# A transformer block pair with expert retrieval on one core: second projections of heads 2 and 3 placed among the first picks, blocks fetched once, head 1's selection earlier, sums on four column tiles

## The reference

```
q = (h2 @ w_query)                       # 8 heads, two halves of 128
s = q . sub_keys                         # 128 scores for each half
v1, i1 = top 16 of half 0; v2, i2 = top 16 of half 1
best = top 16 of all 256 sums v1 + v2    # 16 experts for each token and head
act = gelu(u[expert] . h2)
out += softmax(best) * act * v[expert]
```

## Time and profile before

| | |
|---|---|
| three runs | 1752.94, 1753.07, 1755.21 us (median 1753.07) |
| the profiled execution | 1749.33 us, its span 1747.5 us |
| TensorE matmul busy | 1595.6 us (91%) |
| TensorE weight load busy (beside the matmuls) | 742.7 us (42%) |
| VectorE / ScalarE / GpSimd busy | 750.2 / 500.7 / 288.6 us |
| TensorE's mean granted clock | 0.967 of full |
| moved by DMA | 595.22 MB, mean 341 GB/s |
| SyncE's issues into the ring | 160 (18 of `w_mod` and `w_in`, 142 of packed blocks, of which 8 come in two parts) |
| row fetches from GpSimd | 256 |

### The profile page before, as it was taken

How to read it: one execution, slowest core, us unless ns; L and a number is a source line. 1 busy time by engine, 2 the same in 40 slices (tenths; PEclk the granted TensorE clock), 3 DMA queues, 4 the chain that set the end, 5 groups by cost and what they waited for, 6 DMA issues and landing times.

```text
span 1747.5 us, 15554 instructions
## 1 busy us (share of the span) xinstructions
PE 1595.6 (91%) x5460; PEld 742.7 (42%) x5460; DVE 750.2 (43%) x1807; ACT 500.7 (29%) x1283; POOL 288.6 (17%) x268
## 2 busy tenths in 40 slices
PE   6999998499579997897999988999999999999998
PEld 3444464165134542243443333344344444455443
DVE  3653155866785556646525446542312100031101
ACT  3311224322432323314344134334412110122210
POOL 1000002323533333313212212221000000000000
PEclk8999999799889998999999999999999999999999
DMA  9555349999999999999999999999877677855784
GB/s 353 203 182 193 144 181 382 421 392 421 421 404 410 415 421 421 422 421 421 419 421 420 421 421 421 420 416 421 334 289 272 231 301 269 313 216 226 288 299 181
DMA packets 94958, 595.22 MB, mean 341 GB/s; under 512 B 7025, under 2 KB 7025, under 8 KB 28193
## 3 DMA queue, kind: packets, MB, share of 16 engines
q1 hardware_dynamic: 56576, 319.28, 46.6%
q0 software_dynamic: 37584, 270.75, 37.6%
q10 hardware_dynamic: 720, 4.19, 0.6%
HBM read 593.15 MB, written 1.05 MB: 340 GB/s over the span
## 4 chain that ended last, share of the span: by engine, by line
PE 79%; DMA 11%; DVE 5%; ACT 2%; issue 2%; SPq 1%; POOL 0%; DVEq 0%; POOLq 0%; ACTq 0%
PE bank L975 36%; PE bank L1136 10%; PE bank L1053 8%; DMA arena<-in_peer_rows,pidx 7%; PE bank L684 7%; PE bank L761 3%; PE bank L951 3%; PE bank L940 2%; DMA ring<-in_weights 2%; PE bank L982 2%; DVE arena L2080 2%; DMA ring<-in_w_mod 1%; PE bank L738 1%; PE bank L654 1%; SPq L594 1%
## 5 line engine op out<-in xcount | busy, mean ns | idle before, releaser
L1610 POOL DMA_INDIRECT arena<-in_peer_rows,pidx x227 | 252.3, 1112 | 582.9 <-PE bank L1136 520.7
L1136 PE MATMUL bank<-arena,keep 128*32 128x512 f32 x908 | 264.2, 661 | 71.8 <-ACT keep L1568 71.8
L975 PE MATMUL bank<-ring,arena 128*128 128x512 f32 x736 | 319.4, 593 | 0.0
L2080 DVE SCALAR_TENSOR_TENSOR arena<-arena,ring 128x1024 f32<-128x1024 f32 x227 | 272.6, 1223 | 90.8 <-DMA arena<-in_peer_rows,pidx 88.6
L975 PE MATMUL bank<-ring,hT_all 128*128 128x512 f32 x544 | 239.3, 595 | 3.7 <-issue 3.4
L975 PEld LDWEIGHTS bank<-ring,arena 128*128 128x128 f32 x736 | 138.5, 190 | 168.8 <-issue 168.7
L975 PEld LDWEIGHTS bank<-ring,hT_all 128*128 128x128 f32 x544 | 101.3, 190 | 135.1 <-issue 133.0
L1136 PEld LDWEIGHTS bank<-arena,keep 128*32 128x32 f32 x908 | 50.3, 116 | 215.2 <-issue 119.6
L1555 ACT ACTIVATE pf<-pf 128x2 f32<-128x2 f32 x128 | 25.8, 202 | 374.6 <-DVE arena L2080 334.5
L2195 DVE TENSOR_TENSOR x_all<-x_all,bank 128x512 f32<-128x512 f32 x40 | 27.5, 688 | 205.7 <-PE bank L1053 112.2
L684 PE MATMUL bank<-ring,hT_all 128*128 128x512 f32 x192 | 87.2, 611 | 3.1 <-DMA ring<-in_w_in 1.6
(11 more groups left out here) (374 smaller groups left out, 1704.7 us busy)
## 6 DMA issues: line engine op xcount, KB each, us to landing
ring<-in_weights SPq DMA_DIRECT2D x126, 2048.0 KB
ring<-in_w_mod SPq DMA_DIRECT2D x12, 2048.0 KB
ring<-in_w_in SPq DMA_DIRECT2D x6, 2048.0 KB
ring<-in_weights SPq DMA_DIRECT2D x8, 1024.0 KB
ring<-in_weights SPq DMA_DIRECT2D x8, 512.0 KB
arena<-in_peer_rows,pidx POOLq DMA_INDIRECT x227
mem_all<-in_b_mod POOLq DMA_DIRECT2D x3, 512.0 KB, 9.6
hT_all<-in_xT ACTq DMA_DIRECT2D x1, 1024.0 KB, 7.2
```

Source lines behind the costliest of these rows:

```text
L975: m = mm(b[:, :], src[:, k], slot8[w][:, k], start=(k == 0), stop=(k == KC - 1))
L1136: m = mm(acc[b][r:r + 32, :], diag[n % 8], vslot[n % SLOTS][:, b * 512:(b + 1) * 512], start=(n % 128 < 4), stop=(n % 128 >= 124))
L1610: nc.gpsimd.indirect_dma_start(out=row_in[n % SLOTS], out_offset=None, in_=a["peer_rows"], in_offset=bass.IndirectOffsetOnAxis(ap=pidx[:, ...
L2080: stt(uslot[n % SLOTS], uslot[n % SLOTS], 1.0, h2g[n % 4], ALU.mult, ALU.mult, accum_out=pact2[:, 16 * (g % 2) + k:16 * (g % 2) + k + 1]). ...
```

## The change

It has these parts:

1. `weight_plan` drops `out_again` and `wq_again`. The new order after the modulation and projection blocks is out 1, out 0, wq 0, mod 10, mod 11, wq 1, wq 2, wq 3, in slots 1, 0, 2, 3, 3, 0, 1, 2. A block stays until the second tile has used it: out 0 until the second tile's first half of the projection, out 1 until its second half, wq 0 until query q11, wq 1 until q13.
2. TensorE's stream before the picks loses the queries q02 and q03 and key scores 02 and 03, and gets the second tile's product with out 0 (`out_half(1, 0..3)`) between the transposes mr1 and md1. The modulation rows 10 move up by several steps, and their copy goes to VectorE; that of the transpose at11 goes to ScalarE. The product with out 1 comes at pick 4, q02 at 6, k02 and q03 at 8, k03 at 10.
3. VectorE selects the halves and best pairs of head 1 before the first row products; the rest of head 1 follows after picks 0 to 7, head 2 after picks 10 to 15 (the new table `first`, one entry for each pair).
4. In the sum of a pick pair the second half of the columns goes to partitions 32 * ((n + 2) % 4), so that the four matmuls use four column tiles. `add_experts` reads that half back crosswise in two instructions of 64 partitions.
5. At the start `keep_warm` issues five matmuls of 512 columns whose result nobody reads, and `dist` (1 MB) is issued by SyncE after the fifth block, not by ScalarE as its third DMA.
6. The final norm: the product of the lower half with its gain moves ahead of the last feed-forward product (new step `gain 0`), and on the upper half gain and scale are one instruction.
7. `gate_exp` of groups 1 and 2 moves up on ScalarE.

```diff
-EARLY_PLACES = (0, 1, 2, 0, 1, 3, 1, 2, 0, 1, 2, 0)
+EARLY_PLACES = (1, 0, 2, 3, 3, 0, 1, 2)
...
-    for name, i in (("out", 1), ("out", 0), ("wq", 0), ("wq", 1)):
+    for name, i in (("out", 1), ("out", 0), ("wq", 0)):
         block(name, i)
     rows("mod", 10)
     rows("mod", 11)
-    for name, i in (("out", 1), ("out", 0), ("wq", 0), ("wq", 1)):
-        block(name + "_again", i, name)
-    block("wq", 2)
-    block("wq", 3)
+    for i in (1, 2, 3):
+        block("wq", i)
...
-PICK_WORK = {0: ["out 1"], 4: ["out 0"], 8: ["regroup 1"], 16: ["h2_turns 1"],
+PICK_WORK = {4: ["out 1", "regroup 1"], 6: ["query q02"], 8: ["keys 02", "query q03"], 10: ["keys 03"], 16: ["h2_turns 1"],
...
@@ sync @@
+                if n == 5:
+                    sp.dma_start(s_all[:, 0:2048], a["dist"]).then_inc(sem("dist_in"), 16)
...
-            act.dma_start(s_all[:, 0:2048], a["dist"]).then_inc(sem("dist_in"), 16)
...
@@ tensor @@
+            def keep_warm(n):
+
+                for _ in range(n):
+                    mm(M[0][:, :], ones, h2_all[:, 0:512], start=True, stop=True)
...
             feature_sums("nc", squares_c, sem("squares_ctx"), ones)
+            keep_warm(1)
...
             mod_rows(0, cpad)
+            keep_warm(3)
             mod_rows(2, cpad)
             mod_columns(0)
             mod_columns(2)
+            keep_warm(1)
...
             diff_turn(1, 0)
+            mod_rows(10, cpad)
             ret_values(1, 0)
...
             diff_values(1, 0)
-            mod_rows(10, cpad)
             mod_rows(11, cpad)
...
-            query("q02", 2, slice(0, P))
             pe.wait_ge(sem("mix_ret"), 2)
             turn_blocks(turn("mr1"), [PR[:, 1, c * P:(c + 1) * P] for c in range(4)])
             repeat_tokens(0, 2)
-            key_scores(0, 2)
+            repeat_tokens(0, 3)
+            open_unit("o1a")
+            open_unit("o1b")
+            out_half(1, range(0, 4))
             pe.wait_ge(sem("mix_diff"), 2)
             turn_blocks(turn("md1"), [PR[:, 1, 2048 + c * P:2048 + (c + 1) * P] for c in range(4)])
-            repeat_tokens(0, 3)
-            query("q03", 3, slice(0, P))
-            key_scores(0, 3)
...
-                        r = 32 * (n % 4)
+                        r = 32 * ((n + 2 * b) % 4)
...
@@ vector @@
             mix_ret(1, 2)
+            half_top(1, 0)
+            half_top(1, 1)
+            best_pairs(1)
             out_mean(3)
-            key_copy(0, 2)
+            next_pairs(1)
             mix_diff(1, 3)
-            mix_turn("md", 1)
-            key_copy(0, 3)
...
-                    link(tt(part, acc[half][:, :], g5row[:, c], ALU.mult))
+                    if half == 0:
+                        link(tt(part, acc[0][:, :], g5row[:, c], ALU.mult))
+                    else:
+                        for to, at in ((0, 64), (64, 0)):
+                            q = tt(part[to:to + 64], acc[1][at:at + 64, :], g5row[at:at + 64, c], ALU.mult)
+                        link(q)
...
-            then = {(0, 0): [lambda: half_top(1, 0), lambda: half_top(1, 1)],
-                    (0, 1): [lambda: best_pairs(1), lambda: next_pairs(1), lambda: pair_rows(1, 0), lambda: pair_rows(1, 1), lambda: spread(1), lambda: residual_out(1)],
-                    (0, 2): [lambda: select(1), lambda: h2_mean(1), lambda: half_top(2, 0), lambda: half_top(2, 1), lambda: best_pairs(2), lambda: next_pairs(2)],
-                    (0, 3): [lambda: h2_apply(1), lambda: pair_rows(2, 0), lambda: pair_rows(2, 1), lambda: spread(2)],
+            first = [[lambda: mix_turn("md", 1), lambda: pair_rows(1, 0), lambda: pair_rows(1, 1)], [lambda: spread(1)], [],
+                     [lambda: residual_out(1), lambda: select(1)], [], [lambda: h2_mean(1), lambda: key_copy(0, 2), lambda: half_top(2, 0), lambda: half_top(2, 1)],
+                     [lambda: h2_apply(1), lambda: best_pairs(2), lambda: next_pairs(2)],
+                     [lambda: key_copy(0, 3), lambda: pair_rows(2, 0), lambda: pair_rows(2, 1), lambda: spread(2)]]
...
+                elif kind == "gain":
...
+                    dve.wait_ge(tile_squares[t], i + 1)
+                    low = x[:, t, 0:512]
+                    tt(low, low, frow[:, 0:512], ALU.mult).then_inc(sem("final_gained"), 1)
...
-                    tt(low, low, frow[:, 0:512], ALU.mult).then_inc(sem("final_gained"), 1)
-                    tt(high, high, frow[:, 512:D], ALU.mult).then_inc(sem("final_gained"), 1)
...
-                    ts(high, high, rs, None, ALU.mult).then_inc(sem(f"tile{t}_done1"), 1)
+                    stt(high, high, rs, frow[:, 512:D], ALU.mult, ALU.mult).then_inc(sem(f"tile{t}_done1"), 1)
```

More of the change, by code:

```diff
@@ L233 @@
 for _w, _us, _lag in STEPS:
-    AFTER_ROWS += [(0, _fill) for _fill in FILLS.get(_w, ())] + [(1, _w)]
+    for _fill in FILLS.get(_w, ()):
+        AFTER_ROWS += [(0, "gain 0")] * (_fill == "final 0") + [(0, _fill)]
+    AFTER_ROWS += [(1, "gain 0")] * (_w == "dn1 5") + [(1, _w)]
 SEQUENCE = [(0, _w) for _w in UNDER_ROWS] + AFTER_ROWS
@@ L302 @@
          + [(n, 1) for n in ("at00", "at01", "m4", "m5", "at02", "at03", "m6", "m7", "md0", "mr0")] + [("h20", 2)]
-         + [(n, 1) for n in ("at10", "at11", "m10", "m11", "at12", "at13", "mr1", "md1")] + [("h21", 2)])
+         + [(n, 1) for n in ("at10", "m10", "at11", "m11", "at12", "at13", "mr1", "md1")] + [("h21", 2)])
 def turn(name):
@@ L559, in wait_released @@
                 eng.wait_ge(turn_ready, turn(f"m{i}") + 1)
-            elif (name, i) == ("out_again", 1):
+            elif (name, i) == ("out", 0):
                 eng.wait_ge(sem("out_half_used"), 1)
@@ L731, in out_half @@
             def out_half(t, ks):
+                first, last = (0, 7) if t else (4, 3)
                 for k in ks:
                     if k % 4 == 0:
-                        w = weights(piece["out_again" if t else "out", k // 4])
+                        w = weights(piece["out", k // 4])
                         turned(turn(("mr" if k == 0 else "md") + str(t)))
@@ L738, in out_half @@
                         m = mm(bank[unit(f"o{t}" + "ab"[half]) % 4][:, :], mixT[t][:, k], slot4[w][:, k % 4, half * 512:(half + 1) * 512],
-                               start=(k == 4), stop=(k == 3))
-                        if k == 3:
+                               start=(k == first), stop=(k == last))
+                        if k == last:
                             m.then_inc(unit_ready, 1)
-                        elif k == 7 and half and t:
+                        elif k == 3 and half and t:
                             m.then_inc(sem("out_half_used"), 1)
@@ L751, in query @@
             def query(name, h, cols_of):
-                w = weights(piece["wq_again" if name[1] == "1" and len(name) == 3 else "wq", h // 2])
+                w = weights(piece["wq", h // 2])
                 b = open_unit(name)
@@ L1396, in _ @@
             out_root(3)
-            query_copy("q02", ("k00",))
             mix_turn("mr", 1)
@@ L1400, in _ @@
             repeat_copy(0, 3)
-            query_copy("q03", ("k01",))
+            gate_exp(1)
             def memory_copy(l, u):
@@ L1423, in g5_move @@
                 f(g5row, g5early, ACT.Copy).then_inc(sem("g5_moved"), 1)
-            after = {8: [lambda: h2_square(1)], 10: [lambda: h2_root(1)],
+            after = {6: [lambda: query_copy("q02", ("k00",))], 8: [lambda: h2_square(1), lambda: query_copy("q03", ("k01",))], 10: [lambda: h2_root(1)],
+                     14: [lambda: gate_exp(2)],
                      16: [lambda: h2_turn(1)], 18: [lambda: query_copy("q10")], 20: [lambda: query_copy("q11")],
@@ L1467, in layer_step @@
                       accum_out=ss).then_inc(tile_squares[t], 1)
+                elif kind == "final":
+                    i, ss, ms, sd, rs = tile_stats(t, "final")
                     act.wait_ge(tile_squares[t], i + 1)
@@ L1549, in _ @@
                             repeat_copy(1, i)
-                    if n0 == 8:
-                        gate_exp(1)
-                    if q == 6 and g + 2 < 16:
+                    if q == 6 and 0 < g < 14:
                         gate_exp(g + 2)
@@ L2279, in _ @@
                     dots(n0, n0 + 2)
+                    for work in first[j] if g == 0 else ():
+                        work()
                     if j % 2:
```

27 lines of the change are left out of this document (11 added, 16 removed), and 5 rows, old and new, of tables (UNITS, last_unit).

## The result

The changed kernel takes 1738.49 us in the median of six runs (1737.36 to 1739.77), the kernel before 1753.51 beside it: ratio 0.9914, 95% interval 0.9902 to 0.9927. That is 15 us faster. The forecast was 1729; 1738 is the time given for rival A. The profiled execution took 1737.44 us, its span 1735.6.

What follows compares the result with a forecast made beforehand. DMA bytes were taken to bound the picks until 1128 us, except in windows where TensorE held DMA back, and TensorE after that. 2.5 + 5.5 + 6.2 + 9 + 0.7 = 23.9 us off 1753.1 gave 1729 us, range 1715 to 1742.

Steps and rivals of the forecast that it cites:

- rival A: Stretch after 1128 us: DMA holds it too, so the gain of 9 us goes; 1738 us, chance 18%.
- The start of the picks: From the first row fetch to 350 us: four weight blocks fewer bring 5.5 us (0 to 10).
- the gap: Near 288 us: DMA idles about 3 us because fetches 7 and 8 wait for the transpose md1.
- The two dips: 350 to 370 and 510 to 530 us: shorter sums let DMA regain 2.6 MB, 6.2 us (0 to 7).
- rival D: Picks: TensorE's gaps bring half-clock restarts; after 1128 us they undo the 9 us and cost 6; 1744 us, 5%.
- The last stretch: After 1128 us: TensorE is the bound, 13 shorter sums save 12.0 us, taken as 9 (0 to 12).
- lead of 15 us: After 1128 us: weights up to three blocks, 15 us, ahead of TensorE cover a stretch shorter by 12 us.
- The front: Before the picks: dist moved lands a w_mod block earlier, idle matmuls speed the projection; 2.5 us (0 to 3).
- The final norm: Between mean and reciprocal on VectorE: two products leave this place, gain 0.7 us (0.4 to 1.2).
- B: Picks: bytes count in full, no DMA gap at 287, all 12 us after 1128; 36 us, 1717 us, 14%.
- C: Pair sums: four tiles share the array only in pairs, so their saving is absent; 1744 us, chance 5%.
- E: Picks: 8 us stands with all row slots landed idle DMA; four make it slower, 1761 us, chance 4%.

Runs made afterwards that it cites:

- e1: Changed kernel with the old pair sum on two column tiles and the old add_experts; 1743.88 us, ratio 0.9957 to the kernel before.
- e12: Changed kernel with the transpose md1 moved ahead of the product with out 0; 1733.86 us, ratio 0.9911 to the kernel before.
- e9: Changed kernel with the old two-tile sum for the last 13 pair sums (picks 230 to 255); 1740.00 us, ratio 0.9935 to the kernel before.
- e10: Changed kernel with picks 228 to 243 fetched as 4 KB rows instead of 8 KB; 1729.64 us, ratio 0.9886 to the kernel before.
- e3: Changed kernel without the five idle matmuls and with dist back on ScalarE's queue; 1740.91 us, ratio 0.9945 to the kernel before.
- e6: Changed kernel without the five idle matmuls, dist at its new place; 1737.37 us, ratio 0.9930 to the kernel before.
- the third set: Follow-up runs on one chip, among them the changed kernel unaltered once more: 1738.70 us, ratio 0.9933 to the kernel before.
- e2: Kernel before with only the new four-tile sum and the new add_experts; 1747.96 us, ratio 0.9978 to the kernel before.

## Why the prediction was right in sign and 9 us too low

The sum was 2.5 + 5.5 + 6.2 + 9 + 0.7.

- **The start of the picks, 5.5 forecast:** e1's lead of 5.1 us over its fetch 0 agrees. The byte count held, the gap too: forecast 3 us near 288; measured 221 GB/s at 290 to 295, which is 2.4 us. But it came later than I had it: the product with out 0 began at 284.76 for 283.5 and VectorE's mix_turn at 292.34 for 291, as TensorE ran at half clock before (at 273.39 us 16 records in 3.64 us, which take 1.92 at 278.52). And that gap may be worth more than the 3 us I gave it: e12 removes it and has 3.4 us more in the traces and 0 to 4.8 by the runs. One sentence of this step was wrong at the root: modulation rows 10 moved up "delay" select and cost 0.8 us. I looked at TensorE's and VectorE's order only; the move opens the slot for rows 11, and without it 7.6 us or more are lost. My total escaped this by luck, since I hadn't seen the shared slot either.
- **The two dips, 6.2 forecast:** 350 to 370 is filled, worth 2.7 us of lead in the byte count (4.9 to 7.6). Against e1 it is more: over their own fetch 0 the changed kernel has 9.7 us at fetch 236 and e1 5.0, 4.6 us for the tiles up to there. 510 to 530 isn't: with 290 and 412 GB/s it misses (131 + 9) x 10 us, 1.4 MB or 3.3 us, as much as before. In front of it TensorE stands 7.98 us, and the next product runs at half clock.

```profile
494.02 1.94 PE L1139 MATMUL bank<-arena,keep 128*32 128x512 f32 x8 [7.98 <-ACT keep L1570]
...
500.03 8.75 PE L946 MATMUL bank<-mem_all,ring 128*128 128x256 f32 x32
```

The windows there have 0.50 and 0.67 of the clock. The product takes 8.75 us for 32 records, where the one at 528.62 takes 7.07, and each pair sum 1.94 for 1.07. That is rival D's mechanism, and with it TensorE came to 510 us later than it could have. Whether it is all of the dip wasn't tried; e1, with the old sums, has 335 and 385 GB/s in the same two windows.

- **The last stretch, 9 forecast:** this is the step that failed most. Fetch 236 has 8.9 us of lead, the last sum 11.0: 2.1 us. I took TensorE for the bound behind 1128 because the chain lay on it and because the ring stood full at 1260. The chain named one of two engines that were both full. DMA was at 421 GB/s through the same stretch, and the ring ran ahead only when the last row had been fetched, at 1238: in the earlier trace rows the rate falls after 1250, not before. Of the "lead of 15 us" hardly anything was there at 1130 to 1238: the changed kernel gained 2.1 us and then waited for blocks. e9 and e10 show it from both sides, 2.1 us for 11 us more work and 10.4 us with the bytes gone. Rival A had this, at 18%, and its 1738 is what came; that it came so exactly is luck, as the dips and the front were mis-sized too.
- **The front, 2.5 forecast:** 1.35 us at the `w_mod` row, nothing of it left against the kernel before at 121 us, 0.5 against e3 there, by the runs 2 to 5, not clear of noise. The wait did go: the chain of the changed kernel and that of e6 have no wait for DMA between 15 and 55 us, where the one before has 24.82 us of it. But another path was nearly as late as the block (the norm of the inputs on VectorE, the modulation columns, the projection), so the row came only 1.35 us earlier. The five matmuls bring nothing (e6). In the window of 30 to 40 us the granted clock is 0.72 of full with them, 0.68 without (e6) and 0.83 without (e3). The Trainium skill (TensorE: Matmul & The Clock Gate, Part 1) has activity release the throttle; these rows neither bear that out nor speak against it.
- **The final norm, 0.7 forecast:** 0.9.
- **Rivals B, C, E:** C is out (1.07 us for a sum). B's bytes didn't count in full: there was the gap, and the last stretch gave 2. E's stands were there, 4.82 and 5.85 us on VectorE (ahead of 292.34 and 310.00), but the slots' transfers covered them save for the 2.4 us at 290 to 295.

The traces add up as follows: fetch 0 is 0.8 us late, the start gives 5.0, the tiles 4.6 up to fetch 236 and 2.1 behind it, the tail 0.9; rounding apart these are the 11.9 us by which the spans differ. The split between the start and the tiles rests on e1 and is an estimate. By the runs it is 15 us in the first measurement and 12 in the third set (0.9933).

## What to carry to other kernels

When TensorE and DMA are both full in a stretch, as here from 1160 to 1250 us, the chain can name only one of them, and taking work from it gives what the other had to spare. Ask when a prefetch lead came to be, by the first window in which the rate falls, before you spend it. When a change keeps blocks longer, follow the slots of every block behind them: an innocent move of two us of TensorE work can be what makes the rest possible. And with DMA at the bound, look at the first gap in its windows: swapping two operations on TensorE closed it and gave 3.4 us more in the traces, a quarter of the whole change's gain again.

## What the runs showed of the hardware

- A pair sum of four 128x32 by 512 float32 matmuls takes 1.91 us on two column tiles and 1.07 us on four. This is 0.84 us less, not the 0.92 that two sums in a row had let me expect.
- Less work on TensorE lowered its mean granted clock: 0.967 to 0.934 in the changed kernel and to 0.933 in e2, where only the sums are new; e1, with the old sums, has 0.971. So part of the 108 us that the shorter sums save was given back at 1.2 GHz, and busy time fell by 75 us between e1 and the changed kernel: a pair sum at that level takes 1.94 us (300.27 and 494.02 us), as much as the old one at 2.4.
- At 270 to 280 us the changed kernel shows 0.62 and 0.70 of the clock, where the kernel before had 1.00, after windows with TensorE busy 8 to 10 of 10 us (240 to 270 us) and a wait of 2.36 us ahead of 272.35. What set it off in the changed kernel is open.
